# Differential attention: rotary halves exchanged by transfers instead of products, and another score bank for context queries

## The reference, cut to what matters

```python
def rope(x, pos):                        # second block; d = 64
    ...
    x1, x2 = xf[..., :half], xf[..., half:]
    return jnp.concatenate([x1 * cos - x2 * sin, x2 * cos + x1 * sin], axis=-1)

def diff_attention_group(q, k, v, pos, layer, lambdas, subln):
    ...
    q = rope(q.reshape(bsz, s, 2 * hh, d), pos).reshape(bsz, s, hh, 2, d)
    k = rope(k.reshape(bsz, s, 2 * hh, d), pos).reshape(bsz, s, hh, 2, d)
    ...                                  # per block of 128 queries, chunk-causal mask:
        p1 = masked_softmax(q1 @ k1 * scale, mask)
        p2 = masked_softmax(q2 @ k2 * scale, mask)
        return (p1 - lam * p2) @ v
```

```python
    if need_ctx_out:                     # layer 0 only
        o_ac = _flat(_attend(qa_c, ka_c, va_c, None))
        o_dc = _flat(_attend(qd_c, kd_c, vd_c, sink))
```

## Time and profile before

| | |
|---|---|
| median of 3 runs | 2867.66 us (2867.61 to 2867.77) |
| profiled execution | 2863.03 us, its span 2861.2 us |
| TensorE matmul busy | 2773.6 us, 97% of the span |
| DVE busy | 1369.0 us, 48% |
| ScalarE busy | 848.1 us, 30% |
| GpSimd busy | 1350.7 us, 47% |
| mean granted TensorE clock | 0.990 of full speed |

### The profile page before, as it was taken

How to read it: one execution, slowest core, us unless ns; L and a number is a source line. 1 busy time by engine, 2 the same in 40 slices (tenths; PEclk the granted TensorE clock), 3 DMA queues, 4 the chain that set the end, 5 groups by cost and what they waited for, 6 DMA issues and landing times.

```text
span 2861.2 us, 36702 instructions
## 1 busy us (share of the span) xinstructions
PE 2773.6 (97%) x14560; PEld 2166.2 (76%) x14560; DVE 1369.0 (48%) x2262; ACT 848.1 (30%) x1582; POOL 1350.7 (47%) x1106
## 2 busy tenths in 40 slices
PE   7999999999989999999999999999999999999997
PEld 5988777777878877677797666788787655788886
DVE  3412556666576222434944666524725956511113
ACT  3011432331130134322325354232233234222222
POOL 2445224224534754558765545744545313744433
PEclk9999999999999999999999999999999999999998
DMA  7111222222421122123322212232333311322322
GB/s 271 46 54 58 67 86 80 68 86 81 133 77 60 61 74 73 57 83 120 113 74 67 66 45 74 92 97 87 96 92 113 115 53 39 109 91 89 99 86 75
DMA packets 244836, 243.73 MB, mean 85 GB/s; under 512 B 5392, under 2 KB 234640, under 8 KB 244048
## 3 DMA queue, kind: packets, MB, share of 16 engines
q1 hardware_dynamic: 243376, 237.89, 26.3%
q0 software_dynamic: 1312, 3.80, 0.5%
HBM read 233.16 MB, written 7.34 MB: 84 GB/s over the span
## 4 chain that ended last, share of the span: by engine, by line
PE 87%; DVE 8%; ACT 2%; issue 1%; POOL 1%; SPq 1%; DMA 1%; DVEq 0%; POOLq 0%; ACTq 0%
PE psum L948 23%; PE psum L950 22%; PE psum L949 22%; PE psum L1211 4%; PE psum L1190 1%; PE psum L1146 1%; DVE columns L2679 1%; PE psum L1328 1%; PE psum L1166 1%; PE psum L1487 1%; PE psum L1145 1%; POOL columns L3398 1%; PE psum L1215 1%; PE psum L1507 1%; SPq L785 1%
## 5 line engine op out<-in xcount | busy, mean ns | idle before, releaser
L948 PE MATMUL psum<-columns,columns 128*128 128x512 f32 (+1 forms) x3464 | 1339.7, 387 | 16.0 <-POOL columns L3398 4.9
L950 PE MATMUL psum<-columns,columns 128*128 128x512 f32 (+1 forms) x3464 | 1261.7, 364 | 0.0
L949 PE MATMUL psum<-columns,columns 128*128 128x512 f32 (+1 forms) x3464 | 1260.2, 364 | 0.0
L3398 POOL TENSOR_TENSOR columns<-columns,columns 128x512 fp32r<-128x512 f32 (+1 forms) x676 | 905.3, 1369 | 436.8 <-ACT columns L1881 403.5
L3394 POOL TENSOR_TENSOR columns<-columns,columns 128x512 fp32r<-128x512 f32 x392 | 420.9, 1104 | 965.1 <-PE psum L950 761.3
L948 PEld LDWEIGHTS psum<-columns,columns 128*128 128x128 f32 x3464 | 653.9, 189 | 191.3 <-issue 68.5
L949 PEld LDWEIGHTS psum<-columns,columns 128*128 128x128 f32 x3464 | 654.3, 189 | 122.1 <-issue 25.9
L950 PEld LDWEIGHTS psum<-columns,columns 128*128 128x128 f32 x3464 | 652.9, 188 | 111.3
L1881 ACT ACTIVATE columns<-columns 128x1024 fp32r<-128x1024 f32 (+2 forms) x154 | 136.7, 935 | 172.5 <-PE psum L950 165.8
L2679 DVE SCALAR_TENSOR_TENSOR columns<-columns,columns,columns 128x256 f32<-128x256 f32 x224 | 153.7, 741 | 0.0
L2661 DVE SCALAR_TENSOR_TENSOR columns<-columns,psum 128x512 f32<-128x512 f32 x80 | 54.8, 685 | 188.2 <-PE psum L1211 183.3
(11 more groups left out here) (429 smaller groups left out, 2696.0 us busy)
## 6 DMA issues: line engine op xcount, KB each, us to landing
columns<-in_w_merge SPq DMA_DIRECT2D x32, 1024.0 KB, 6.8
columns<-in_w_ada SPq DMA_DIRECT2D x24, 1024.0 KB, 5.4
columns<-in_w_in SPq DMA_DIRECT2D x22, 1024.0 KB, 5.4
columns<-in_ev_w_in SPq DMA_DIRECT2D x22, 1024.0 KB, 5.3
columns<-in_ffn_gate SPq DMA_DIRECT2D x22, 1024.0 KB, 5.3
columns<-in_ffn_up SPq DMA_DIRECT2D x22, 1024.0 KB, 5.3
columns<-in_ffn_down SPq DMA_DIRECT2D x16, 768.0 KB, 4.8
columns<-in_ffn_down SPq DMA_DIRECT2D x16, 640.0 KB, 4.5
```

The lines of the kernel that those rows point to most:

```text
L948: mm(dst, weights(0, k), moving(0, k), start=start and k == 0, stop=False)
L949: mm(dst, weights(0, k), moving(1, k), start=False, stop=False)
L950: last = mm(dst, weights(1, k), moving(0, k), start=False, stop=stop and k == k_tiles - 1)
L3398: last = g.tensor_tensor(low[:, c], raw[:, c], high[:, c].bitcast(F32), ALU.subtract)
```

## The change

1. Rotary halves: after its copy to `raw2`, ScalarE waits for it and issues four transfers of 32 partitions x 512 float32 (64 KB each) from `raw2` to a new tile `swap2`, which exchange neighbouring groups of 32 partitions. The `swap` product, its matrix in the constants and its use of bank 2 are gone. DVE reads `swap2` in place of PSUM, at k = 6 in place of 4. There are two semaphores for arrivals, by parity of the tile.
2. The cosine product signals `cosined`, and tile n + 2 waits for that instead of `roped`. The first output tiles wait likewise, and the third waits for nothing.
3. Context queries: the second head's scores go to bank 5, and the wait between the two products is gone.
4. A semaphore of the second block (`dt_turned`) is merged into `dt_sum`.

```diff
 def score_columns(b, t, h):
     n_x = unit_keys(b, t)[1]
-    return (SCORES_AT + BANK - n_x if h < 2 else SCORES_AT + BANK + CTX), n_x + CTX
+    return SCORES_AT + BANK + (-n_x if h < 2 else CTX if n_x else BANK), n_x + CTX
...
-ROPE_AT, EXPS, TURN, MIX, LAST_WEIGHTS = 4, 2, 8, 11, UNIT_STARTS[-1] + 5
+ROPE_AT, EXPS, TURN, MIX, LAST_WEIGHTS = 6, 2, 8, 11, UNIT_STARTS[-1] + 5
...
-        raw2 = take(2, SEQ, at=5120)
+        raw2, swap2 = take(2, SEQ, at=5120), take(2, SEQ, at=2048)
...
-                        context_at = SCORES_AT + BANK + c * CTX
+                        context_at = SCORES_AT + BANK + c * (CTX if n_x else BANK)
...
                         scores(0, False).then_inc(scored, 1)
-                        pe.wait_ge(scored, base + u + 1)
                     scores(1, False).then_inc(scored, 1)
...
-                def swap(n):
-                    pe.wait_ge(raw_ready, n + 1)
-                    if n:
-                        pe.wait_ge(roped, n)
-                    mm(psum[:, 2 * BANK:3 * BANK], c2("swap32"), raw2[:, n % 2, :], start=True, stop=True).then_inc(swapped, 1)
...
-                    if k == ROPE_AT and 1 <= n <= 16:
-                        swap(n - 1)
...
                             else:
-                                pe.wait_ge(roped, n - 1)
+                                pe.wait_ge(cosined, n - 1)
...
-                            if t < 3:
-                                pe.wait_ge(roped, min(15 + t, 16))
-                            else:
+                            if t < 2:
+                                pe.wait_ge(cosined, 15 + t)
+                            elif t >= 3:
                                 pe.wait_ge(half_added, t - 2)
...
                         f(raw2[:, i % 2, :], psum[:, i % 2 * BANK:(i % 2 + 1) * BANK], ACT.Copy, ...).then_inc(raw_ready, 1)
+                        act.wait_ge(raw_ready, i + 1)
+                        for b in range(4):
+                            act.dma_start(swap2[32 * b:32 * b + 32, i % 2, :], raw2[32 * (b ^ 1):32 * (b ^ 1) + 32, i % 2, :]).then_inc(swapped[i % 2], 16)
...
                 def rope(n):
-                    x, swp = qk2[:, qk_tile(n), :], psum[:, 2 * BANK:3 * BANK]
-                    dve.wait_ge(swapped, n + 1)
+                    x, swp = qk2[:, qk_tile(n), :], swap2[:, n % 2, :]
+                    dve.wait_ge(swapped[n % 2], 64 * (n // 2 + 1))
+                    dve.wait_ge(cosined, n + 1)
                     order(v.tensor_tensor(swp, swp, sind, ALU.mult))
                     v.tensor_tensor(x, swp, x, ALU.add).then_inc(roped, 1)
```

More of the change, by code:

```diff
@@ L71 @@
               ("conv_w", 48), ("conv_b", 12), ("d_skip", 8), ("gate_norm", 8), ("subln", 1), ("lambdas", 256),
-              ("swap32", 128), ("swap_mla", 128), ("rot_c", 128), ("sub_sums", 64),
+              ("swap_mla", 128), ("rot_c", 128), ("sub_sums", 64),
               ("dt_bias", 1), ("a_log", 1), ("reset", 512), ("s5_skip", 4), ("b_glu", 4), ("q_norm", 3), ("kv_norm", 2),
@@ L653, in build @@
         dt_ready = sem("dt_ready")
-        dt_turned = sem("dt_turned")
         x_turned_used = sem("x_turned_used")
@@ L663, in build @@
         roped = sem("roped")
-        swapped = sem("swapped")
+        swapped = [sem("swapped0"), sem("swapped1")]
+        cosined = sem("cosined")
         v_ready = sem("v_ready")
@@ L1375, in ev_xbc @@
                         mm(psum[:, 6 * BANK + 192:6 * BANK + 256], ones2[0:16, :], dlx[0:16].rearrange("p c h -> p (c h)"),
-                           start=True, stop=True).then_inc(dt_turned, 1)
+                           start=True, stop=True).then_inc(dt_sum, 1)
             def ev_vz():
@@ L2866, in ev_xbc @@
                     if n == 9:
-                        dve.wait_ge(dt_turned, 1)
+                        dve.wait_ge(dt_sum, 2)
                         v.tensor_copy(cols[:, 40:44], psum[:, 6 * BANK + 256:6 * BANK + 260]).then_inc(token_scales, 1)
@@ L2931, in cosines @@
                     dve.wait_ge(raw_ready, n + 1)
-                    order(v.scalar_tensor_tensor(out=qk2[:, qk_tile(n), :], in0=psum[:, n % 2 * BANK:(n % 2 + 1) * BANK],
-                                                 scalar=0.125 if is_query(n) else 1.0, in1=cosd, op0=ALU.mult, op1=ALU.mult))
+                    v.scalar_tensor_tensor(out=qk2[:, qk_tile(n), :], in0=psum[:, n % 2 * BANK:(n % 2 + 1) * BANK],
+                                           scalar=0.125 if is_query(n) else 1.0, in1=cosd, op0=ALU.mult, op1=ALU.mult).then_inc(cosined, 1)
                 def rope(n):
-                    x, swp = qk2[:, qk_tile(n), :], psum[:, 2 * BANK:3 * BANK]
-                    dve.wait_ge(swapped, n + 1)
+                    x, swp = qk2[:, qk_tile(n), :], swap2[:, n % 2, :]
+                    dve.wait_ge(swapped[n % 2], 64 * (n // 2 + 1))
+                    dve.wait_ge(cosined, n + 1)
                     order(v.tensor_tensor(swp, swp, sind, ALU.mult))
@@ L3586, in tables2 @@
     a, b = np.arange(P)[:, None], np.arange(P)[None, :]
-    s32, smla, rot = (np.zeros((P, P), np.float32) for _ in range(3))
-    for p in range(P):
-        s32[p ^ 32, p] = 1
+    smla, rot = (np.zeros((P, P), np.float32) for _ in range(2))
     for p in range(P):
@@ L3618, in tables2 @@
         "lambdas": np.broadcast_to(g("ev_lambdas_2").reshape(1, 256), (P, 256)),
-        "swap32": s32, "swap_mla": smla, "rot_c": rot, "tri": np.where(b >= a, 0, NEG).astype(np.float32), "sel": sel, "sub_sums": sub_sums,
+        "swap_mla": smla, "rot_c": rot, "tri": np.where(b >= a, 0, NEG).astype(np.float32), "sel": sel, "sub_sums": sub_sums,
         "dt_bias": rows(g("ev_dt_bias_2")), "a_log": rows(g("ev_a_log_2")), "reset": reset,
```

## The result

The changed kernel takes 2883.70 us (median of 4 runs, 2880.43 to 2884.46), the kernel before beside it 2867.64 (4 runs, 2862.57 to 2867.77): a ratio of 1.0062 on record, 95% interval 1.0049 to 1.0074 (the two medians alone give 1.0056). It is slower by 16.1 us, where no change was forecast, and the time lies above the range. The profiled execution has a span of 2882.6 us against 2861.2, and a mean granted clock of 0.982 against 0.990.

What follows compares the result with a forecast made beforehand. TensorE's own work, 87% of the span, was taken as the bound. Gains 10.9 + 0.4 + 6.0 = 17.3 us less stalls 17.3 gave net 0.0: 2867.7 us, range 2854.5 to 2875.

Steps and rivals of the forecast that it cites:

- Context queries: Context pairs' two score products overlap in one bank: 0.75 us each, 8 pairs, gain 6.0 us (bounds 3.7 and 6.0).
- rival 5: Context pairs don't overlap, only the wait between them goes: 3.7 in place of 6.0, 2870.0 us; chance 0.05.
- Transfers' landing: Rotary exchange: 64 KB transfers land after 1.9 to 4.1 us, median 2.6, covered within 0.3 us before DVE's rotation.
- Rival 4: Exchange transfers land late, one after another, so DVE and TensorE are late in five tiles: +10, 2877.7 us; chance 0.05.
- What ScalarE takes on: Behind each raw copy: four issues at 0.42 us and 0.1 for the wait, 1.8 us per tile; exp 1.9 later.
- rival 3: ScalarE pays GpSimd's 0.54 us per issue, 2.5 per tile, 0.7 more at 11 stalls: +7.7, 2875.4 us; chance 0.13.
- The stalls: TensorE waiting for late ScalarE in the attention stage: 1.9 + 1.0 + 4 x 1.9 + 4 x 1.2 + 2.0 = 17.3 us.
- step 0 of the period: First tile of a 16-step, two-tile attention period: margin zero, stall 1.9 us four times; first period margin 0.9, stall 1.0.
- step 8: Second tile of a 16-step attention period: exp ends past unit 1's score start, stall 1.2 us, four times.
- rival 2: Issues of 0.18 to 0.25 us, or a stall leaves room at the next: -5.5 to -8.8, about 2860.5; chance 0.15.
- The four tiles before the first head cost TensorE nothing: Attention stage's first four tiles: no scores stand behind them, so ScalarE's delay there adds no stall.
- Swaps removed: Swap products off TensorE: 0.84 us each, 13.4 for 16, 13 counted, gain 10.9; the 0.4 wait before L948 also goes.

Runs made afterwards that it cites:

- the version with the sines first: Against the changed kernel: DVE multiplies by the sines from PSUM before the exchange, no raw copy, cosine product left in PSUM, transfers issued from SyncE; 2853.83 us, ratio 0.9957.
- The kernel with swaps kept and idle transfers: Kernel before plus the context queries' second scores in the next bank; swaps stay products, 64 ScalarE transfers (four per tile) added that nobody reads; 2891.51 us, ratio 1.0092.
- the bank change: Kernel before with only the context queries' second scores moved to the next bank and the wait between the two products removed; 2857.11 us, ratio 0.9973.
- the kernel with one idle transfer: Kernel before plus the context queries' second scores in the next bank; swaps stay products, one unread ScalarE transfer per tile added; 2862.12 us, ratio 0.9989.

## Why the prediction failed

In the stage the forecast had +6.0 us (stalls 17.3, less 10.9 and 0.4), measured is +22.4. Of the 16.4 us between, waits make 6.8 (23.7 against 16.9) and the clock 12.1, by what is left over; that the swaps gave back 13.4 and not 10.9 takes 2.5 off. Two steps failed: the price of an issue, and a clock taken as constant.

- **Context queries**: right. 6.3 us at the merge's load against 6.0; rival 5 falls.
- **Transfers' landing**: right. 1.9/2.0/4.1 us against 1.9/2.6/4.1; DVE waited for one once, 4.1 us at the first tile. Rival 4 falls. That holds for this kernel alone: where the same transfers were issued later, or from SyncE, DVE waited for them 10.0 and 14.2 us in all.
- **What ScalarE takes on**: the first step that failed. I took SP's 0.37 us, from a load of a weight panel, for an issue of a transfer from columns to columns, and left GpSimd's 0.54, the one row with the same operands, to rival 3. Measured is 0.61 in place of 0.42, and 2.57 us from the copy's end to exp, not 1.8. It isn't ScalarE's own price either: SP, with the same transfers in the version with the sines first, shows the line below, beside its 0.37 for panels. The kind of transfer sets the price, not which of these two engines issues it; what in the kind does it (SBUF as the source, the 32 partitions, the size) no run separates.

```profile
L858 SPq DMA_DIRECT2D columns<-columns x64: 507/591/1258, 1567.2 to 1719.0; - x64
```

- **The stalls**: the margins at step 0 of the period were right, the sizes followed the price. There the stall is the whole delay, 2.64, 3.15, 2.65 and 2.65 us (forecast 1.9 each); in the first period 2.22 (1.0), at the first head 2.79 (1.9). At step 8 it is 0.62 to 0.64 four times and not 1.2: a stall at one tile leaves room at the next, as rival 2 said. At the end of the stage it is 1.9 us more than before (2.0). TensorE's waits for L2150 and L2210 went to 22.6 us in all, where the forecast's sign was about 17.
- **"The four tiles before the first head cost TensorE nothing"**: wrong. They cost 3.7 us of waits for DVE (0.73, 1.21, 1.78), two of them for the cosine product, whose 0.4 us the forecast had as gone. I had the slow two-operand operation in hand, 1.61 us beside GpSimd, and used it at step 8 alone; before the first head DVE stands beside GpSimd's passes too, and has no idle time there.
- **The clock**: the second step that failed. It is missing from the sum, put at nothing without a reason, and by what is left over it is the largest part of the miss. A period took 20.45 us before (1654.26 to 1674.71 for L1517) and takes 23.57 after (1688.55 to 1712.12 for L1510): 3.1 longer, not 1.4. Waits give 3.3, swaps -1.7, so 1.5 is slower products. The kernel with swaps kept and idle transfers has the same waits in a period of 23.69 us, 20.45 + 3.27 being 23.72, and its windows show the full clock (PEclk, the third from the right):

```profile
1640.00:1660.00 20.00, 19.37 (x96) 13.58 (x95) 12.64 (x25) 7.24 (x21) 5.49 (x5) 1.00 0.23 68
1660.00:1680.00 20.00, 16.79 (x91) 11.74 (x91) 10.57 (x23) 8.90 (x25) 7.12 (x7) 1.00 0.26 78
1680.00:1700.00 20.00, 16.72 (x90) 11.53 (x86) 11.61 (x23) 8.42 (x23) 9.21 (x8) 1.00 0.28 80
```

  So in these periods, once the waits are there, what the removed swaps gave back went into the clock. TensorE does less between the same waits; more than that no run shows.
- **Swaps removed** as 10.9 us: borne out only where DVE reads PSUM (9.5 us in the medians, 11.9 in the stage). In the change as made nothing of it comes through.
- Rival 3, slower by a dear issue, had the mechanism, with 2.5 us of delay per tile, and gave 2875.4 at 0.13, just outside the range that was to take in most of it. The 8 us still missing are the clock and the first tiles, less the smaller stalls at step 8 and the swaps' other 2.5.

In medians: the bank change -8.1 (2865.2 to 2857.1); swaps gone -9.5 (2847.6); DVE's reads from SBUF +11.5 (2859.2); ScalarE's hold with the clock behind it +24.5 (2883.7; 24.4 by the ratios).

## What to carry to other kernels

Price an issue by a row of the same kind of transfer (here SBUF to SBUF over 32 partitions, about 0.6 us), and count it against the engine's next instruction that someone waits for: four issues put ahead of the exponentials cost 24 us, the same four behind them 4. When an operand moves from PSUM to SBUF, look at who else works there: the same DVE operation was 0.69 us from PSUM and up to 1.8 with both operands from SBUF. When several waits of about 2 us and more come in, ask what TensorE's clock does behind them, and don't count on what it saves between them.

## What the runs showed of the hardware that was not expected

- Issues of these transfers take 0.51 us singly and 0.61 in a row of four from ScalarE, 0.59 from SP.
- In the changed kernel the products behind waits of 2.2 us and more took 0.63 us in place of 0.40 for some 3 us, and before the first head, where it began behind waits of up to 1.8 us, for about 10 (the level of 1.2 GHz in place of 2.4; granted clock 0.68 to 0.91 over five of the windows of 20 us). The same waits with 0.84 us more of products for each tile between them left it at 1.00 from 1620 to 1700, as did waits of 0.7 us in the kernel with one idle transfer (1640 to 1700).
- Four transfers of 64 KB, the first issued 0.4 us behind a 1 MB load on SP's queue, kept DVE waiting 5.7 us. The median of the 64 landed in 2.1 us, the slowest in 5.3.
